# Expert (PEER) stages of a three-block fp32 model: held-back weight loads, and a first projection half done by token block

## What is computed

```python
def peer_ffn(h, wq, k1, k2, u_tab, v_tab):
    hb = h.reshape((B * S) // 128, 128, D)
    def block(xb):
        q = (xb @ wq).reshape(128, 8, 2, 128)
        s1 = jnp.einsum('phd,kd->phk', q[:, :, 0], k1)
        s2 = jnp.einsum('phd,kd->phk', q[:, :, 1], k2)
        v1, i1 = lax.top_k(s1, 16)
        v2, i2 = lax.top_k(s2, 16)
        cand = v1[..., :, None] + v2[..., None, :]        # 256 candidates a head
        top_s, top_pos = lax.top_k(cand, 16)              # 16 experts a head
        g = jax.nn.softmax(top_s, axis=-1)
        act = jax.nn.gelu(jnp.einsum('pd,phkd->phk', xb, u_tab[eid]))
        return jnp.einsum('phk,phkd->pd', g * act, v_tab[eid])
    return lax.map(block, hb)
...
for l in range(2):                                        # first block
    x = x + g1 * mixer(rmsnorm(x) * (1 + sc1) + sh1, ...)
    x = x + g2 * peer_ffn(rmsnorm(x, norm_ffn[l]) * (1 + sc2) + sh2, ...)
x = rmsnorm(x, final_norm)                                # then blocks two and three
```

## Time and profile before

| | us |
|---|---|
| median of 3 runs | 3965.23 (3957.39 to 3965.59) |
| the profiled execution | 3969.06 |
| its span | 3967.3 |
| PE busy | 3320.0 (84%) |
| DVE busy | 2040.7 (51%) |
| POOL busy | 1031.0 (26%) |
| ACT busy | 926.2 (23%) |
| gathers of `u_rows`, `v_rows` | 512 + 512, 536.94 MB |
| mean DMA rate over the span | 240 GB/s |

### The profile page before, as it was taken

One profiled execution on the slowest core, in us unless ns is written; L12 is line 12 of the kernel. 1 busy time (PEld: TensorE's weight loads), 2 busy tenths in 40 slices (PEclk: granted clock), 3 DMA queues, 4 the chain that ended last, 5 costly groups with the idle time before them and its releaser, 6 DMA issues. The chain is left out here.

```text
span 3967.3 us, 33939 instructions
## 1 busy us (share of the span) xinstructions
PE 3320.0 (84%) x12000; PEld 2185.2 (55%) x12000; DVE 2040.7 (51%) x3682; ACT 926.2 (23%) x1557; POOL 1031.0 (26%) x1090
## 2 busy tenths in 40 slices
PE   5896577778887577777998999999998988999798
PEld 3663222223663222223876787875687878654387
DVE  5567766654547766655534545433455435302254
ACT  0211111110112111112422434302443312101143
POOL 0026777763016777764000000000000001100000
PEclk9799899999899899999998999998999989999899
DMA  9379999998449999996541555541455533343353
GB/s 365 135 263 383 409 409 409 409 395 329 178 166 383 409 409 409 409 406 262 191 162 64 169 184 167 175 149 64 162 188 165 181 127 108 102 163 107 127 180 116
DMA packets 402037, 951.13 MB, mean 240 GB/s; under 512 B 30652, under 2 KB 171488, under 8 KB 401632
## 3 DMA queue, kind: packets, MB, share of 16 engines
q0 software_dynamic: 147456, 536.94, 34.2%
q1 hardware_dynamic: 245088, 397.09, 29.4%
q10 hardware_dynamic: 9344, 15.22, 1.1%
HBM read 948.06 MB, written 1.07 MB: 239 GB/s over the span
## 5 line engine op out<-in xcount | busy, mean ns | idle before, releaser
L1395 PE MATMUL PS<-v_rows,xn 128*128 128x512 f32 x1944 | 911.0, 612 | 372.6 <-DMA v_rows<-in_peer_v_dram,peer_ids 368.2
L1395 PEld LDWEIGHTS PS<-v_rows,xn 128*128 128x128 f32 x1944 | 355.9, 193 | 926.5 <-issue 592.4
L1470 DVE CUSTOM_DVE_ANT_0 u_rows<-u_rows,PS 128x1024 f32<-128x1024 f32 x512 | 621.8, 1220 | 358.6 <-DMA u_rows<-in_peer_u_dram,peer_ids 330.7
L702 DVE TENSOR_TENSOR ring_lo<-ring,ring_hi 128x2048 fp32r<-128x2048 f32 x198 | 452.8, 2292 | 260.3 <-ACT ring_hi L641 259.8
L1534 POOL DMA_INDIRECT u_rows<-in_peer_u_dram,peer_ids x512 | 485.2, 948 | 281.8 <-issue 145.7
L1534 POOL DMA_INDIRECT v_rows<-in_peer_v_dram,peer_ids x512 | 488.3, 954 | 166.8 <-issue 143.9
L641 ACT CAST ring_hi<-ring 128x2048 fp32r<-128x2048 f32 x198 | 376.8, 1912 | 287.4 <-PE PS L558 156.2
L558 PE MATMUL PS<-ring_hi,hT_hi 128*128 128x512 f32 x1056 | 421.2, 399 | 16.4 <-DVE hT_lo L742 12.1
L440 PE MATMUL PS<-hT,ring 128*128 128x256 f32 x1920 | 423.4, 382 | 2.7 <-PEq L347 1.5
L558 PE MATMUL PS<-ring_hi,hT_lo 128*128 128x512 f32 x1056 | 414.9, 393 | 0.0
L558 PE MATMUL PS<-ring_lo,hT_hi 128*128 128x512 f32 x1056 | 414.8, 393 | 0.0
(11 more groups left out here) (366 smaller groups left out, 2898.4 us busy)
## 6 DMA issues: line engine op xcount, KB each, us to landing
ring<-in_ffn_w_gate_dram SPq DMA_DIRECT2D x132, 512.0 KB, 3.7
ring<-in_ffn_w_up_dram SPq DMA_DIRECT2D x132, 512.0 KB, 4.7
ring<-in_ffn_w_down_dram SPq DMA_DIRECT2D x66, 1024.0 KB, 4.9
ring<-in_w_in_dram SPq DMA_DIRECT2D x64, 1024.0 KB, 4.9
ada_ring<-in_ada_w_dram SPq DMA_DIRECT2D x96, 512.0 KB, 8.2
ring<-in_peer_wq_dram SPq DMA_DIRECT2D x16, 1024.0 KB, 5.2
ring<-in_c_w_in_dram SPq DMA_DIRECT2D x14, 1024.0 KB, 4.9
ring<-in_w_out_dram SPq DMA_DIRECT2D x8, 1024.0 KB, 11.1
```

The costliest lines, as they stand in the source:

```text
L702: nc.vector.tensor_tensor(halves(c)[1], slot, halves(c)[0], ALU.subtract).then_inc(S.w_lo, 1)
L1395: ins = nc.tensor.matmul(self.PS[:, 2 * b + h, :], diag[:, r % NDIAG, :], rowsV[:, m % VRING, h * BANK:(h + 1) * BANK], start=(n % (slots ...
L1470: ins = nc.vector.tensor_tensor_reduce(rowsU[:, m % URING, :], rowsU[:, m % URING, :], H[b], 1.0, 0.0, ALU.mult, ALU.add, dots[:, e:e + 1])
```

## The change

Three things are changed, all in the two PEER stages.

1. SP waits, before it issues the first chunk of the next stage, until v row `(l + 1) * slots - 4` has landed, that is slot 252 of 256 (`slots` is 256; counted over both layers).
2. Mean square, power and scaling are done per token block, each with its own signal. DVE still sums the squares of both blocks before it scales block 0. The tiles of block 0 count on a semaphore of their own, `n_hT0`, and PE waits for these two groups alone before its first half.
3. Half 0 of part 0 is done first for the 128 tokens of block 0, then its scores, then for block 1; `back(0)` comes after that, then half 1, the scores of block 1, and the scores of half 1. ACT copies the half block by block.

```diff
@@ load_weights
             self.load_side(sp, min(due, side_last))
+            if hold and n == end:
+                sp.wait_ge(*hold)
             if n >= RING:
                 sp.wait_ge(self.w_used, n - RING + 1)
@@ peer, stage
+                    hold=slot_landed(self.v_landed, VRING, (l + 1) * slots - 4)) as (block, S):
@@ peer, tensor
-                    pe.wait_ge(S.n_hT, self.N_HT)
                     wq = [self.take(pe).rearrange("p (k n) -> p k n", k=4) for _ in range(2)]
-                    for e in range(2):
+
+                    def half(e, lo, hi):
+
                         for k in range(KT):
                             for t in range(2):
                                 c = (2 * e + t) * P
-                                ins = nc.tensor.matmul(self.PS[:, e, t * SEQ:(t + 1) * SEQ], wq[k // 4][:, k % 4, c:c + P],
-                                                       self.hT[:, k, :], start=(k == 0 and t == 0), stop=(k == KT - 1),
+                                ins = nc.tensor.matmul(self.PS[:, e, t * SEQ + lo:t * SEQ + hi], wq[k // 4][:, k % 4, c:c + P],
+                                                       self.hT[:, k, lo:hi], start=(k == 0 and t == 0 and lo == 0), stop=(k == KT - 1),
                                                        skip_group_check=True)
...
+                    pe.wait_ge(S.n_hT0, 2)
+                    half(0, 0, P).then_inc(S.half, 1)
+                    pe.wait_ge(S.keysT_out, 1)
+                    pe.wait_ge(S.queries, 1)
+                    scores(0, 0, 2, [0])
+                    pe.wait_ge(S.n_hT, 2)
+                    half(0, P, SEQ).then_inc(S.half, 1)
+                    back(0)
+                    half(1, 0, SEQ).then_inc(self.w_used, 2)
+                    pe.wait_ge(S.queries, 2)
+                    scores(0, 0, 2, [1])
+                    pe.wait_ge(S.queries, 3)
+                    scores(0, 2, 4)
@@ peer, scalar
-                    act.wait_ge(S.half, 1)
-                    queries(0, 0)
-                    nc.scalar.drain().then_inc(S.queries, 1)
-                    collect(0, 0, 2, 0)
+                    for b in range(NB):
+                        act.wait_ge(S.half, b + 1)
+                        ins = nc.scalar.copy(QT[:, 0, 0:2, b * P:(b + 1) * P],
+                                             self.PS[:, 0, :].rearrange("p (t n) -> p t n", t=2)[:, :, b * P:(b + 1) * P])
+                        if b == 1:
+                            ins.then_inc(S.p_free0, 1)
+                        nc.scalar.drain().then_inc(S.queries, 1)
+                        collect(0, 0, 2, 0, [b])
                     self.leave(act, 0)
                     queries(0, 1)
@@ peer, vector
-                    self.norm_vector(ve, S, self.modA[:, 1, :], shift)
+                    for b in range(NB):
+                        nc.vector.tensor_tensor_reduce(self.xn[:, b, :], self.X[:, b, :], self.X[:, b, :], 1.0 / D, EPS,
+                                                       ALU.mult, ALU.add, self.ms[:, b:b + 1])
+                        nc.vector.drain().then_inc(S.n_ms, 1)
+                    for b in range(NB):
+                        ve.wait_ge(S.n_rstd, b + 1)
+                        nc.vector.tensor_scalar(self.xn[:, b, :], self.X[:, b, :], self.rstd[:, b:b + 1], None,
+                                                ALU.mult).then_inc(S.n_xn, 1)
+                    self.evacuate_tiles(ve, nc.vector, S, 1, self.modA[:, 1, :], shift, S.n_hT0)
@@ peer, gpsimd
-                    self.norm_gpsimd(pool, S)
+                    for b in range(NB):
+                        pool.wait_ge(S.n_ms, b + 1)
+                        nc.gpsimd.tensor_tensor(self.rstd[:, b:b + 1], self.ms[:, b:b + 1], self.neghalf[:, b:b + 1], ALU.pow).then_inc(S.n_rstd, 1)
```

More of the change, by code:

```diff
@@ L253, in plan, with load_weights @@
         self.issued = self.taken = 0
-    def load_weights(self, sp, name, side=None):
+    def load_weights(self, sp, name, side=None, hold=None):
         end = self.chunk_end.get(name, self.taken)
@@ L339, in stage @@
     @contextmanager
-    def stage(self, names, weights=None, side=None):
+    def stage(self, names, weights=None, side=None, hold=None):
         nc = self.nc
@@ L354, in _ @@
                 def _(sp):
-                    self.load_weights(sp, weights, side)
+                    self.load_weights(sp, weights, side, hold)
             yield block, namedtuple("StageSemaphores", names)(*mine[:len(names)])
@@ L391, in norm_tensor, with evacuate_tiles @@
                 ins.then_inc(S.n_tr, 1)
-    def evacuate_tiles(self, eng, ops, S, odd, scale, shift):
+    def evacuate_tiles(self, eng, ops, S, odd, scale, shift, first=None):
         for b in range(NB):
@@ L410, in evacuate_tiles @@
                         ins = ops.activation(out, src, ACT.Identity, bias=bias, scale=scale[:, k:k + 1])
-                ins.then_inc(S.n_hT, 1)
+                ins.then_inc(first if first is not None and b == 0 else S.n_hT, 1)
     def norm_scalar(self, act, S, scale, shift):
@@ L1222, in columns, with slot_landed @@
                 return slice(TOPK * work[p][1], TOPK * (work[p][1] + work[p][2]))
+            def slot_landed(sem, ring, m):
+                return sem[m % ring], 16 * (m // ring + 1)
             tail = [n for n in range(slots - TAIL, slots) if n % 3 == 2]
@@ L1316, in peer @@
             with self.stage(
-                    "n_ms n_rstd n_xn n_tr n_hT p_free0 p_free1 back keysT keysT_out half scores score_out "
-                    "queries shifted expd ids dots gelu weights diag tail", f"peer_q{l}") as (block, S):
+                    "n_ms n_rstd n_xn n_tr n_hT0 n_hT p_free0 p_free1 back keysT keysT_out half scores score_out "
+                    "queries shifted expd ids dots gelu weights diag tail", f"peer_q{l}",
+                    hold=slot_landed(self.v_landed, VRING, (l + 1) * slots - 4)) as (block, S):
                 QT = self.sb("peer_qT", [P, 2, LISTS, SEQ], ctx=ctx)
@@ L1330, in peer @@
                 used = l * -(-len(summed) // 2)
-                def slot_landed(sem, ring, m):
-                    return sem[m % ring], 16 * (m // ring + 1)
                 def collected(b, h):
@@ L1341, in _, with scores @@
                 def _(pe):
-                    def scores(j, first, last):
-                        for b in range(NB):
+                    def scores(j, first, last, blocks=range(NB)):
+                        for b in blocks:
                             for i in range(first, last):
@@ L1367, in _ @@
                                 c = (2 * e + t) * P
-                                ins = nc.tensor.matmul(self.PS[:, e, t * SEQ:(t + 1) * SEQ], wq[k // 4][:, k % 4, c:c + P],
-                                                       self.hT[:, k, :], start=(k == 0 and t == 0), stop=(k == KT - 1),
+                                ins = nc.tensor.matmul(self.PS[:, e, t * SEQ + lo:t * SEQ + hi], wq[k // 4][:, k % 4, c:c + P],
+                                                       self.hT[:, k, lo:hi], start=(k == 0 and t == 0 and lo == 0), stop=(k == KT - 1),
                                                        skip_group_check=True)
[L1371 to L1378, removed]
+                        return ins
+                    pe.wait_ge(S.n_hT0, 2)
[11 more added lines that the diff above has]
+                    scores(0, 2, 4)
                     for j in range(1, parts):
                         self.project(pe, S, [("F", 512)], self.hT, KT, first=j)
-                        pe.wait_ge(S.queries, j + 2)
+                        pe.wait_ge(S.queries, j + 3)
                         pe.wait_ge(S.score_out, 2 * j + 2)
@@ L1405, in _ @@
                         act.dma_start(keys[:, i, :], a[name][l]).then_inc(side, 16)
-                    self.norm_scalar(act, S, self.modA[:, 1, :], shift)
+                    self.evacuate_tiles(act, nc.scalar, S, 0, self.modA[:, 1, :], shift, S.n_hT0)
                     def queries(j, e):
@@ L1409, in queries, with collect @@
                                        self.bank(j, e)).then_inc(self.freed(S, j), 1)
-                    def collect(j, first, last, count):
-                        for b in range(NB):
+                    def collect(j, first, last, count, blocks=range(NB)):
+                        for b in blocks:
                             act.wait_ge(S.scores, count + b + 1)
```

## The result

The changed kernel took 3975.52 us (median of 7 runs, 3972.49 to 3978.19); the kernel before, in the same comparison, 3963.55 (7 runs, 3957.39 to 3973.01). The ratio is 1.003 [1.0018, 1.0042], about 12 us slower. The number lies in the range of the prediction, but "no change" was the likeliest case there; what came is, in the main, the third rival, the burst at the end of layer 1 that nothing covers. On another chip, where the kernel before takes 4130.57 us, the same change was 0.3% faster.

What follows compares the result with a forecast made beforehand. Each PEER stage's head was taken as bound by PE's projections with ACT behind them, the rest by DMA. +1.0 (PE's chain) +0.4 (last rows) +1.3 (gain) +0.4 (SP) = +3.1 on 3965.2: 3968.3 us, range 3953 to 3977.

Steps and rivals of the forecast that it cites:

- no change: Whole kernel: time the same, as a measurement tells some 0.2% (7.9 us) from no change; chance 0.63.
- the third rival: Final norm after layer 1: gain behind all six chunks, +6.3; SP's issue holds the stage another 2; about +10, 3975; chance 0.16.
- The hole is a barrier: DMA idle before item 2's gathers, both layers: later gathers wait for item 2's ids, so earlier transfers gain nothing.
- Rivals one and two: Gather phases: the first says gathers shorten by the 15.4 us of weights a layer, -31, 3934, chance 0.10; second: see rival two.
- rival two: Both PEER stages: the head start carries through if the gelu comes earlier too; -5 a layer, 3955; chance 0.10.
- PE's chain: PE's work ahead of item 0's gelu: +0.2 in layer 0, both layers together +1.0, bounds -3 and +4.
- DVE's wait: Before the first weighing: the wait for the gelu grows from 9.94 to near 15 us, costed at nothing.
- The clock in layer 1: Layer 1's first half, beginning at 1139.9: its first 1.1 us run at PE's low clock, +0.6.
- Layer 0's end: Last rows of layer 0's stage beside the new loads: +0.2, bounds 0 and +1.8; the chunks' arrival covered by residual and norm.
- SP's issue: Stage ends: a stage ends only when SP has issued its burst; +0.4, bounds 0 and +3.
- The gain: Final norm after layer 1: the gain's load shares the DMA with weight loads in equal turns; +1.3, between 0 and +6.3.

Runs made afterwards that it cites:

- hold alone: The kernel before plus SP's wait before the next stage's weight chunks, in both layers, nothing else: 3972.91 us, ratio 1.0018 [1.0007, 1.0028].
- reorder alone: The changed kernel without SP's wait; norm and first half by token block stay: 3964.95 us, ratio 0.9999 [0.9988, 1.0011].
- the gelu was moved: Item 0's gelu put ahead of the last projection part's copies, slower chips: on the kernel before 0.993 and 0.9932, on the changed one 0.9919.
- the early gain: The changed kernel with the final norm's gain loaded at the start of layer 1's PEER stage: 3970.91 us, ratio 1.001 [0.9997, 1.0022].

## Why the prediction was right or wrong

**Right, with the numbers in its own terms:**
- *The hole is a barrier.* Neither 15.4 us of transfer taken out (hold alone: stages +0.2 and -0.6) nor a first gather 5 us earlier (reorder alone: -0.7 and -1.1) shortened a stage by over 1.1 us. Rivals one and two (-31, and -5 a layer) are out on the first chip. On the slower chips rival two came true in part, once the gelu was moved; its condition, that the gelu comes earlier too, was named.
- *PE's chain.* Start of the first half after the stage's first DVE instruction 9.07 to 7.45: -1.6, as forecast. Two halves 7.50 for 7.17: +0.3 (+0.6 forecast). ACT's copy before the scores: 0.57 (0.6). Behind half 1: PE waits 0.99 for 0.71. The first project begins at 26.25 for 26.79, -0.5 where I had +0.2; item 2 -0.5 and +0.2 us where I had +0.2 and +0.8. That is 0.7 and 0.6 us a layer better, inside the bounds.
- *DVE's wait* was forecast near 15 us, the weighing at 80 to 82: 13.2, 13.4 and 79.8, 80.4. DVE came to its wait 3.8 and 3.2 us earlier, not 5.
- *The clock in layer 1.* PE began the first half at 1140.39 there, with a granted clock of 0.50 until 1141.7, and it took 4.36 us against 3.76 in layer 0: the +0.6 forecast for it.
- *Layer 0's end.* SP issued its six chunks in 8.40 us from 946.84, the stage ended at 956.63, the next opened 0.42 later. Held open by nothing, as forecast.

**Wrong: two terms at the end of layer 1**, which the forecast of "no change" hung on.
- *SP's issue, taken at +0.4 with bounds 0 and +3; measured +3.7, and +2.4 with the hold alone.* I had the only burst of six chunks in the trace of before, 10.54 us, and set SP's end "about" the stage's. The start was right: the burst begins 9.9 us before DVE ends (9.6 by my count). Its length was not: the eleven transfers need 13.5 us, since SP's issue falls back to the pace of the data, and 13.5 - 9.9 is the 3.6 us by which SP outlasts DVE. With the hold alone, in the same place, they need 12.2 us. The upper bound was short for the changed kernel and held for the hold alone.
- *The gain, taken at +1.3 between 0 and +6.3; measured +3.4.* It was issued at 1866.55 instead of 1858.93, held up by the first term, and met some 2.4 MB of loads (2.92 MB moved from then to 1876, the gain's 0.52 taken off). By the page of the Trainium skill that I cited, "DMA: Bandwidth & Descriptors", section "Queues, rings and completion order", turns are taken packet by packet. The transfer landed 7.0 us after its issue against 3.6 alone: +3.4, more than equal turns and less than coming last. How the turns fell is not shown.

These two are 7.1 us of trace time, 6.0 with the hold alone, and 3.8 of them went with the early gain. The third rival had both at this place and priced them at +6.3 for the gain and +2 for the issue; the runs have +3.4 and +3.7, with the hold alone +3.5 and +2.4. Its total of about +10 is close to the +12 [+7, +17] measured, partly by luck, since neither part was. What stands between 7 and 12 is not settled: 3 us of it may be the drop of PE's clock in layer 1, if most runs have it, and that was in no term. The mistake was not the mechanism but the size of the two terms and the chance of the rival: both sat in the same 16 us with a slack of nothing, and I took each at the low end of its bounds.

A slip without effect on the sum: at the 409 GB/s that it reads, a MB is worth 2.44 us, not 2.56; the 15.4 us for 6.29 MB are right.

**Not foreseen at all:** that the sign depends on the chip.

## What to carry to other kernels

A head start is worth what the next barrier lets through: find the wait that ends last between the gain and the end, and move that first. A transfer moved out of a busy stretch must land in a stretch with slack, and its *issue* counts too: where all engines meet at a stage's end, count the issuing engine's time at the pace of the data, not at the pace of its first few transfers, and look at which small transfer now queues behind the big ones. Before a difference of 0.3% is called a property of a kernel, run it on a second chip.

## What was not expected of the hardware

- SP issued the first four 0.52 MB transfers of a burst in 0.37 to 0.78 us each, and the seven later ones, 4.2 MB, in 11.1 us, with the DMA engines at a share of 1.0 to 1.1. The issue was held back to the rate of the data.
- Chips ran the same kernel 4% apart (3966 us on one, 4139 and 4131 on two others), nearly all of it in the gather stages. On the slower ones PE, ACT and DVE stopped at full stretches of gathers, PE for 1 to 2.3 us between single matmuls, DVE for up to 9.6 us, and the gathers came to 370 GB/s against 406. Each chip was seen in one session alone.
- A drop of PE's granted clock to 0.50 for 3 us went with 3 us more of stage where gathers waited for the slots that PE frees, twice, and cost nothing to be seen where the DMA engines were full.
- A 128-row fp32 record of 128 columns took 3.76 us for 32, 0.1175 each, against 0.22 for one of 256 columns: a moving side half as wide cost slightly more than half.
